# Attention by pairs of heads, side by side in the TensorE array, in one core's decoder step

## What is computed

```python
def sparse_core(q, k_sel, v_sel, valid):   # 8 heads of 64
    s = einsum("bthd,btkhd->bthk", q, k_sel) * 64 ** -0.5
    p = softmax(where(valid, s, -inf)); return einsum("bthk,btkhd->bthd", p, v_sel)
def mem_attend(qm, mk, mv):                # 4 heads of 128, 256 memory tokens
    s = einsum("bthd,bmhd->bthm", qm, mk) * 128 ** -0.5
    p = softmax(s); return einsum("bthm,bmhd->bthd", p, mv)
```

## Time and profile before

| what | value |
|---|---|
| median of 3 runs | 2982.36 us (2980.09 to 2985.59) |
| the profiled execution | 2974.08 us |
| its span, first to last instruction | 2972.5 us |
| mean granted TensorE clock | 0.988 of full speed |
| attention in the profile | about 1610 to 1947 us from the start of the span |

### The profile page before, as it was taken

How to read it: one execution, slowest core, us unless ns; L and a number is a source line. 1 busy time by engine, 2 the same in 40 slices (tenths; PEclk the granted TensorE clock), 3 DMA queues, 4 the chain that set the end, 5 groups by cost and what they waited for, 6 DMA issues and landing times. The chain is left out here.

```text
span 2972.5 us, 56828 instructions
## 1 busy us (share of the span) xinstructions
PE 2844.4 (96%) x21242; PEld 2709.4 (91%) x21242; DVE 2341.1 (79%) x3873; ACT 1236.1 (42%) x2373; POOL 1137.3 (38%) x808
## 2 busy tenths in 40 slices
PE   6999989999999999999988999999989999899999
PEld 6999989999899999999986777799889999899999
DVE  8888897777758999999985666547378888977776
ACT  5444444444433333233445555521344443443443
POOL 4555545554543331113321000021355555454552
PEclk8999999999999999999998999999999999999999
DMA  4333323332232222223128777634533333233331
GB/s 160 93 93 93 104 75 93 93 92 87 86 80 87 87 87 75 85 58 95 59 89 298 265 238 253 227 121 137 148 101 99 100 93 101 75 103 98 95 98 57
DMA packets 359407, 340.35 MB, mean 114 GB/s; under 512 B 16831, under 2 KB 293666, under 8 KB 359134
## 3 DMA queue, kind: packets, MB, share of 16 engines
q1 hardware_dynamic: 354430, 330.41, 35.9%
q0 software_dynamic: 4128, 4.20, 0.5%
q10 hardware_dynamic: 576, 2.10, 0.2%
HBM read 299.60 MB, written 37.05 MB: 113 GB/s over the span
## 5 line engine op out<-in xcount | busy, mean ns | idle before, releaser
L294 PE MATMUL bank<-op_r_ffn,w_hi 128*128 128x256 f32 (+1 forms) x2992 | 580.8, 292 | 32.4 <-DVE op_r_ffn L275 18.2
L294 PEld LDWEIGHTS bank<-op_r_ffn,w_hi 128*128 128x128 f32 x2992 | 475.5, 191 | 39.1 <-issue 36.5
L294 PE MATMUL bank<-op_r_ffn,w_lo 128*128 128x256 f32 (+1 forms) x1496 | 433.5, 290 | 0.0
L294 PE MATMUL bank<-h_hi,w_hi 128*128 128x362 f32 (+1 forms) x1272 | 422.2, 332 | 6.8 <-ACT qi L2024 2.6
L435 POOL TENSOR_TENSOR w_lo<-sums_ffn,w_hi 128x512 fp32r<-128x512 f32 x214 | 317.7, 1494 | 264.5 <-ACT w_hi L431 264.5
L294 PE MATMUL bank<-h_lo,w_hi 128*128 128x362 f32 (+1 forms) x1272 | 417.9, 329 | 0.0
L294 PE MATMUL bank<-h_hi,w_lo 128*128 128x362 f32 (+1 forms) x1272 | 417.8, 328 | 0.0
L294 PE MATMUL bank<-op_r_ffn,more_hi_ffn 128*128 128x288 f32 (+1 forms) x1936 | 375.0, 291 | 13.9 <-ACT s_ffn L575 5.3
L294 PEld LDWEIGHTS bank<-op_r_ffn,more_hi_ffn 128*128 128x128 f32 x1936 | 306.3, 190 | 17.8 <-issue 8.5
L435 POOL TENSOR_TENSOR more_lo_ffn<-sums_ffn,more_hi_ffn 128x512 fp32r<-128x512 f32 x138 | 203.2, 1480 | 226.4 <-ACT more_hi_ffn L431 226.4
L294 PEld LDWEIGHTS bank<-op_r_ffn,w_lo 128*128 128x128 f32 x1496 | 286.0, 191 | 0.0
(11 more groups left out here) (429 smaller groups left out, 7141.8 us busy)
## 6 DMA issues: line engine op xcount, KB each, us to landing
raw<-in_w_ffn_in SPq DMA_DIRECT2D x132, 512.0 KB, 3.9
raw_ffn<-in_w_ffn_out SPq DMA_DIRECT2D x88, 512.0 KB, 3.5
v_ring<-in_cache_v SPq DMA_DIRECT2D x128, 256.0 KB, 4.7
raw<-in_w_in SPq DMA_DIRECT2D x53, 512.0 KB, 4.9
raw_ffn<-in_w_ffn_in SPq DMA_DIRECT2D x44, 512.0 KB, 3.8
kt_two<-in_cache_k SPq DMA_DIRECT2D x88, 256.0 KB, 3.6
kept_g<-stage SPq DMA_DIRECT2D x24, 544.0 KB, 3.1
gate<-kept_g SPq DMA_DIRECT2D x24, 544.0 KB, 3.7
```

The source lines that it names most:

```text
L294: mm = pe.matmul(out, left, right, start=(start and i == 0 and j == 0), stop=(stop and i == n - 1 and j == 2))
```

## The change

A step is now a "double": one query tile with two heads (prompt), or two query tiles with one head (memory). There are 48 of them, and 12 of them are two heads with their memory part.

- Scores: the two heads stand in the upper and lower 64 rows of the array (`tile_position=(e * DH, 0)`), each with its own banks (0 and 1, or 2 and 3). Three products (high by high, high by low, low by high) take the place of two per head. All four banks belong to one double, and the scores of a double wait for the reading of the one just before it.
- Values: the two heads stand in the left and right 64 columns of the array (`tile_position=(0, e * DH)`), the values being the stationary operand now and 128 columns of transposed probabilities the moving one. The output comes out transposed, so that `oturn` falls away.
- The reciprocals of the row sums have to be transposed instead. DVE takes the reciprocals (entry `invert`), copies them over 64 or 128 columns each (`inv`), PE transposes that (entry `inverse`, one block, or two for memory), ACT or DVE copies it to `inv_t`, and DVE multiplies the output by it.
- Turns come one step after the scores, where they came two steps after, and values two steps after, where they came three steps after. They take banks 4 and 7, and 1 and 3 too where these are free.
- The sample's operations: one sample per 6 doubles, in three places of a step: between scores and values, between values and turns, and after the turns' exponential.
- The parts of queries and keys are made for two heads at once, over 128 rows. `vp` has one buffer. Scratch tiles of the stage before (`spread_q`, `mk_sq`) are moved, and the first branch products of the merge wait for other semaphores.

```diff
-    jobs = []
-    for h in range(H):
-        jobs += [("att", i, h) for i in (0, 7, 1, 6, 2, 5, 3, 4)] + [("mem", h % 2 * 4 + i, h // 2) for i in range(4)]
+    doubles = []
+    for hp in range(H // 2):
+        doubles += [("att", i, 2 * hp) for i in (0, 7, 1, 6, 2, 5, 3, 4)] + [("mem", 2 * m, hp) for m in range(4)]
     slots = [
-        [],
-        [("sc", 0)],
-        [("sc", 1)],
-        [("sc", 2)],
-        [("sc", 3)],
-        [("sc", 4), ("smax",)],
-        [("soft",), ("msc",)],
-        [("pt", 0), ("pt", 1), ("pt", 2), ("pt", 3), ("pt", 4)],
-        [("pv",), ("mpt",)],
-        [("mpv",), ("ot",)],
-        [("mot",)],
-        [],
+        ([], [("sc", 0)], []),
+        ([("sc", 1)], [("sc", 2)], []),
+        ([("sc", 3)], [("sc", 4), ("smax",)], []),
+        ([], [("soft",), ("msc",)], []),
+        ([("pt", 0), ("pt", 1), ("pt", 2), ("pt", 3), ("pt", 4)], [("pv",)], [("mpt",)]),
+        ([("mpv",)], [("ot",)], [("mot",)]),
...
+    def sample(d, place):
+        if d < n:
+            for e in slots[d % 6][place]:
+                add(d, e[0], d // 6, *e[1:])
+
+    n = len(doubles)
+    add(0, "queries", 0)
+    add(0, "keys", 0)
+    for d in range(n + 2):
+        if d < n:
+            add(d, "scores", d)
+            following = d // 12 + 1
+            if d % 12 == 8 and following < H // 2:
+                add(d, "queries", following)
+            if d % 12 == 9 and following < H // 2:
+                add(d, "keys", following)
+        sample(d, 0)
+        if 0 <= d - 2 < n:
+            add(d, "values", d - 2)
+        if n <= d:
+            add(d, "merge", 2 + 2 * (d - n))
+        sample(d, 1)
+        if 0 <= d - 1 < n:
+            blocks = 2 * (doubles[d - 1][1] + 1) if doubles[d - 1][0] == "att" else 4
             for g in range(0, blocks, 4):
-                add("turn", s - 2, g, min(4, blocks - g))
-        if s < n:
-
-            add("exp", s)
-            following = s // 12 + 1
-            if s % 12 == 8 and following < H:
-                add("keys", following)
-            for e in slots[s % 12]:
-                add(e[0], s // 12, *e[1:])
-            if s % 12 == 7 and following < H:
-                add("queries", following)
-    return jobs, plan
+                add(d, "turn", d - 1, g, min(4, blocks - g))
+            add(d, "invert", d - 1)
+        if d < n:
+            add(d, "exp", d)
+        sample(d, 2)
+        if 0 <= d - 1 < n:
+            add(d, "inverse", d - 1)
+        if d == n - 1:
+            add(d, "merge", 0)
+            add(d, "merge", 1)
+        elif d == n:
+            add(d, "merge", 3)
...
+    vp = place("vp", [P, 8, P], F32, 0)
+    vn = place("vn", [DEC_T, 512], F32, 4096)
...
+    pb = [place("pb_even", [P, SEQ], F32, 32768), place("pb_odd", [P, 2 * SEQ], F32, 36864)]
...
+    for entry, turn, step in plan:
+        if entry[0] == "scores" and wide(step):
+            held_at[step] = {b: held[b] for b in (1, 3) if b in held}
+        if turn is None:
+            continue
+        free = (4, 7) if wide(step) or step < 2 or step >= n - 3 else (4, 7, 1, 3)
...
+        elif kind == "inverse":
+            d = entry[1]
+            w = 1 if doubles[d][0] == "att" else 2
+            if d >= 1:
+                eng.wait_ge(normed, d)
+            copy(inv_t[:, 0:w, :], b[:, 0:w * P].rearrange("p (e n) -> p e n", e=w)).then_inc(evicted[me], 1)
...
+    def values_of(sp, hp):
+        if hp == 0:
             after_heads(sp, "heads_summed")
-        if j >= 2:
-            sp.wait_ge(valued, last_of["att", 2 * j - 3] + 1)
+        else:
+            sp.wait_ge(valued, last_att(hp - 1) + 1)
         v_rows = O["new_v_prompt"][0, 0].rearrange("(t p) h d -> p t (h d)", p=P)
-        sp.dma_start(vp[:, j % 2, :, :], v_rows[:, :, j * P:(j + 1) * P]).then_inc(vp_in[j % 2], 16)
+        sp.dma_start(vp[:, :, :], v_rows[:, :, hp * P:(hp + 1) * P]).then_inc(vp_in, 16)
...
+                d = s
+                what, i, h = doubles[d]
+                if d >= 1:
+
+                    pe.wait_ge(*scores_read(d - 1))
                 if what == "mem":
-                    if s == 8:
+                    if d == 8:
                         pe.wait_ge(mk_gained, 1)
-                    mm = pe.matmul(bank[b0][:, 0:N_MEM], qmT[:, h, i * P:(i + 1) * P], mkT[:, h, :],
-                                   start=True, stop=True)
+                    for e in range(2):
+                        mm = pe.matmul(scores_of(d, e), qmT[:, h, (i + e) * P:(i + e + 1) * P], mkT[:, h, :],
+                                       start=True, stop=True)
                 else:
                     keys = (i + 1) * P
                     if i == 0:
-                        pe.wait_ge(k_low, 2 * (h + 1))
-                        pe.wait_ge(q_low, h + 1)
+                        pe.wait_ge(q_low, h // 2 + 1)
+                        pe.wait_ge(k_low, h // 2 + 1)
                     for c, k0 in enumerate(range(0, keys, 512)):
                         w = min(512, keys - k0)
-                        out = bank[b0 + c][:, 0:w]
-                        pe.matmul(out, qq[:, i * P:(i + 1) * P], kk_hi[:, k0:k0 + w], start=True, stop=False)
-                        mm = pe.matmul(out, qq[:, i * P:(i + 1) * P], kk_lo[:, k0:k0 + w], start=False, stop=True)
+                        if c:
+                            for t in held_at[d].values():
+                                wait_turn(pe, t)
+                        for m, (q_, k_) in enumerate(((q_hi, k_hi), (q_hi, k_lo), (q_lo, k_hi))):
+                            for e in range(2):
+                                r = slice(e * DH, (e + 1) * DH)
+                                mm = pe.matmul(bank[2 * e + c][:, 0:w], q_[r, i * P:(i + 1) * P], k_[r, k0:k0 + w],
+                                               start=(m == 0), stop=(m == 2), tile_position=(e * DH, 0))
...
                     for j in range(i + 1):
-                        mm = pe.matmul(bank[6][:, 0:DH], pt[:, j, :], vp[:, h // 2 % 2, j, h % 2 * DH:(h % 2 + 1) * DH],
-                                       start=(j == 0), stop=(j == i))
+                        for e in range(2):
+                            r = slice(e * DH, (e + 1) * DH)
+                            mm = pe.matmul(bank[6][r, 0:P], vp[:, j, r], pt[:, e * (i + 1) + j, :], start=(j == 0),
+                                           stop=(j == i), tile_position=(0, e * DH))
...
+            elif kind == "inverse":
+                d = s
+                pe.wait_ge(spread, d + 1)
+                for e in range(1 if doubles[d][0] == "att" else 2):
+                    mm = pe.transpose(tb[:, e * P:(e + 1) * P], inv[:, e, :], ident[:, :])
                 mm.then_inc(turned, 1)
             elif kind == "sc":
...
+    def split_low(dve, hp):
+        dve.wait_ge(q_high, hp + 1)
+        dve.tensor_tensor(q_lo[:, :], qT[:, hp, 0:SEQ], q_hi[:, :].bitcast(F32), ALU.subtract).then_inc(q_low, 1)
+        dve.wait_ge(k_high, hp + 1)
+        dve.scalar_tensor_tensor(k_lo[:, :], kT[:, hp, 0:SEQ], gains[:, 0:1], k_hi[:, :].bitcast(F32),
+                                 ALU.mult, ALU.subtract).then_inc(k_low, 1)
...
+            elif kind == "invert":
+                d = s
+                c = col(d, 0)
+                dve.wait_ge(exped, 2 * d + 2)
+                if d >= 1:
+                    dve.wait_ge(turned, turn_of[("inverse", d - 1)] + 1)
+                dve.reciprocal(rinv[:, c:c + 2], rsum[:, c:c + 2]).then_inc(inverted, 1)
+                dve.wait_ge(inverted, d + 1)
+                if doubles[d][0] == "att":
+                    dve.tensor_copy(inv[:, 0, :].rearrange("p (e n) -> p e n", e=2),
+                                    rinv[:, c:c + 2].unsqueeze(2).to_broadcast([P, 2, DH])).then_inc(spread, 1)
+                else:
+                    dve.tensor_copy(inv[:, :, :], rinv[:, c:c + 2].unsqueeze(2).to_broadcast([P, 2, P])).then_inc(spread, 1)
...
+                dve.wait_ge(valued, d + 1)
+                wait_turn(dve, turn_of[("inverse", d)])
+                to, w = (qT[:, h // 2, i * P:(i + 1) * P], P) if what == "att" else (qmT[:, h, i * P:(i + 2) * P], 2 * P)
+                dve.tensor_tensor(to, bank[6][:, 0:w], inv_t[:, :, :].rearrange("p e n -> p (e n)")[:, 0:w], ALU.mult).then_inc(normed, 1)
```

More of the change, by code:

```diff
@@ L2827, in attention_plan, with add @@
     turns = 0
-    def add(*entry):
+    def add(step, *entry):
         nonlocal turns
         turn = None
-        if entry[0] in ("turn", "oturn", "pt", "mpt", "ot", "mot"):
+        if entry[0] in ("turn", "inverse", "pt", "mpt", "ot", "mot"):
             turn = turns
             turns += 1
[L2835 to L2840, removed]
-        if s < n:
[L2842 to L2858, removed]
-            for g in range(0, blocks, 4):
-                add("turn", s - 2, g, min(4, blocks - g))
-        if s < n:
-            add("exp", s)
-            following = s // 12 + 1
-            if s % 12 == 8 and following < H:
```

(39 more changed lines are left out.)

304 lines of the change are left out of this document (130 added, 174 removed).

## The result

| | before | after |
|---|---|---|
| median of the timed runs, side by side on one chip | 2981.23 us (2975.26 to 2985.59, 4 runs) | 3004.03 us (3001.89 to 3005.60, 4 runs) |
| ratio after / before | | 1.008, 95% interval 1.0068 to 1.0093 |
| span of the profiled execution | 2972.5 us | 3000.3 us |
| mean granted clock of the profiled execution | 0.988 | 0.984 |
| first scores to first merge product, in the profile | 1610.4 to 1939.9: 329.5 us | 1610.6 to 1967.3: 356.8 us |

The changed kernel is slower by 22.8 us (0.8%). In the profiles all of the difference, 27.3 of 27.8 us, lies in attention.

What follows compares the result with a forecast made beforehand. Attention was taken as bound by PE, the PE, DVE, ACT chain close behind. Terms +13 (stage), -1.5, +2 and +1 gave +14.5 on 2974.1, 2988.6; with 8.3 for the median, 2997 us, range 2956 to 3026.

Steps and rivals of the forecast that it cites:

- rival 3: Attention: idle stretches in 12 places each bring a spell at the 1.2 GHz clock, +12 us, 3009 us; chance 0.10.
- PE's work: Attention, per two heads: PE's work falls from 73 to 64.3 us by values, scores and changes of array division.
- Values: Prompt values: two heads' passes run side by side, 72 pairs at 0.11 us, -7.9 us per two heads.
- Scores with their changes of division: Prompt scores: three sets of passes for four, -2.2 us per two heads; all changes of array division together, +1.4.
- the question that I left between two values: Score weight loads of two half-tiles: overlapping they give 8.6 us over the kernel, queued only 2.2.
- Rival 4: Attention: the array's halves don't run side by side, +26 us for scores and +32 for values, 3055 us; chance 0.05.
- The new wait: Before `inverse`, PE waits 1.35 us for DVE's copy, reciprocal and copy; with other waits 19 us per two heads.
- step 9: Tenth of each 12 steps: ACT needs 7.6 us where PE has 3.5, so PE waits 4.1 us.
- step 2: Third of each 12 steps: PE waits 1.7 us for ACT's exponential and 2.3 for `smax`, 4.0 together.
- the fourth key group: Sample's key load: about 7 us of lead against some 6 of issue and landing; 0 to +8, taken as +1.
- Ends of the stage: Attention's start, up to the first `pv`, -1.5 us; its end, with merge operations on ACT and low parts, +2 us.
- Rival 1: Attention: DVE and ACT run ahead, waits stay near 12 us per two heads, 2969 us (2949 without more waits); chance 0.25.

Runs made afterwards that it cites:

- values_in_line: Changed kernel with the prompt's values of the first head all ahead of those of the second, same products: 3017.87 us, ratio 1.0133 to the kernel before.
- filler: Changed kernel with 2 to 20 unread identity transposes per step put on PE ahead of the wait for the reciprocals: 3006.18 us, ratio 1.0084 to the kernel before.
- late_two_banks: Changed kernel with the reciprocals' transposes one step later and memory doubles' scores alternating between banks 0 and 2: 2969.50 us, ratio 0.9961 to the kernel before.
- late_inverse: Changed kernel with the transposes of the reciprocals one step later, between the next scores and values: 2986.18 us, ratio 1.0025 to the kernel before.
- scores_in_line: Changed kernel with the first head's three score products all ahead of the second's, per 512 key columns: 3007.72 us, ratio 1.0081 to the kernel before.
- copy_twice: Changed kernel with DVE copying the prompt doubles' reciprocals to `inv` twice (32 more copies of 0.227 us): 3020.59 us, ratio 1.0136 to the kernel before.

## Why the prediction was right, and where it was short

The forecast was 2997, slower, in a range of 2956 to 3026; it is 3004, between the forecast and the 3009 of rival 3, the clock. Against the kernel before, +14.5 was forecast and +22.8 measured.

**PE's work.** Forecast -8.7 per two heads, measured -8.8 at full clock. Values were forecast at -7.9, and their share of the sum over starts goes from 20.5 to 12.9, -7.6. Scores with their changes of division: forecast -2.2 and part of +1.4; measured 12.1 to 10.9. The pace is as put there, 0.23 for 512 columns of both heads:

```profile
1750.99 0.19 PEld L3185 LDWEIGHTS bank<-k_low,q_high 64*128 64x128 f32 x2
1751.23 0.19 PEld L3185 LDWEIGHTS bank<-k_high,q_low 64*128 64x128 f32 x2
1751.46 0.19 PEld L3185 LDWEIGHTS bank<-k_high,q_high 64*128 64x128 f32 x2
1751.69 0.19 PEld L3185 LDWEIGHTS bank<-k_low,q_high 64*128 64x128 f32 x2
1751.80 0.19 PEld L3185 LDWEIGHTS bank<-k_high,q_low 64*128 64x128 f32 x2
```

These rows decide the question that I left between two values. In the last two rows the pair of one product starts 0.11 us after the pair of the one before: two half-tiles of 128 columns go in what one full load took the earlier trace rows. The Trainium skill, "TensorE: Matmul & The Clock Gate", section "LDWEIGHTS (loading the stationary operand)", has a load's time go with its columns and not its rows. Whether or not that rule holds for each load, the two don't queue. Rival 4 is out: for the scores by these rows, for the values by what taking their overlap away cost, some 16 us (values_in_line).

**The new wait.** Forecast: 1.35 us basic, some 55 us for all `inverse`. Measured from the start of PE's last operation ahead of `inverse` to that of `inverse`, less one pass of 0.11, 48 times: 54.9 us. By step: 3 and 6 forecast 1.4, measured 1.4; 10 and 11 1.2, measured 1.3; 8 2.7, measured 2.6; 4, 5 and 7 0.9, measured 0.9, 0.3, 0.9. In step 9, 4.1 forecast; 1.5 and 1.6 in the rows above, 1 less. Two other terms were wrong and about cancel, which is luck. In step 2, I had 1.7 for `sc` 4 behind ACT's exponential and 2.3 for `smax`, 4.0 together; PE waits 1.4 for `inverse` and 0.3 for ACT's copy, some 9 us less over the stage. Against that the fourth key group, put at +1 from 0 to 8, costs 8.9 (6.8 and 2.1, four places of 1.5 to 3.5 us; before there was no such wait): the lead of 7 us over 6 of issue and landing was too thin.

**What was short: the clock.** I priced it as a rival, at +12 for the stage, and kept it out of the forecast. In the profile 47.6 us are at the 1.2 GHz level where 13.6 were, in nine spells instead of three that begin in the stage (the last of each runs on past its end). The six in mid-stage begin in or shortly behind a stretch of 1.8 to 2.7 us in which PE started nothing, though not every such stretch is followed by one. One of them, the 12 us around the two waits of steps 8 and 9:

```profile
1762.00:1774.00 12.00, 6.53 (x50) 4.46 (x48) 7.98 (x14) 7.41 (x17) 0.00 (x0) 0.86 0.79 257
```

What a spell makes longer is the work in it (the transposes above, 0.20 apart instead of 0.12), not the waiting for another engine. The distances from start to start, waits left out, sum to about 18 us in the eight spells ahead of the merge's products, against 3.2 in two before, and half of the difference, about 7 us, is lost. The timed runs point the same way. Of 107 executions of 13 kernels each has a span and a mean clock; within a kernel, one that has 0.001 less clock is 2.1 us longer (correlation -0.77). The kernel before has 0.9866 on the mean of 41, the changed one 0.9817 of 4: 10 us by that slope, an estimate. So the clock makes up 7 to 10 of the 22.8 us, by estimate, and with the forecast's 14.5 that is about the result. Two caveats: a slope within kernels isn't an experiment on the clock, since a run that waits longer can have a lower clock for that very reason, and filler, which was to be one, didn't move it enough. I count this part as supported, not as shown.

**Where the rest went.** Ends of the stage: forecast -1.5 and +2, in the profiles +2.1 to the first `pv` (in it stands one of the waits for a key page, 3.5 us) and +2.7 after the last (the last `inverse` waits 2.7, and the first merge product 3.9 for POOL's low part, where it waited 1.2). So in the profiles, where the difference is 27.3 us and not 22.8, the ends took 4 us more than forecast and the clock 7, which is most of the excess over 14.5. DVE's 46 us per two heads came out at 45.4; it isn't a bound by volume.

**The sign.** Rival 1 (faster) was to turn at 15.7 us of waits per two heads, in the forecast's way of counting. late_two_banks is that rival made true by two edits, some 12 us faster than the kernel before, a third of the 35 that no more waits than before would have given. The later `inverse` alone wasn't enough for the sign (1.0025, with an interval above 1); it took the second bank as well.

## What to carry to other kernels

When a faster form of a product needs a small product more (here a transposed reciprocal), ask what PE does between the last operation that it waits for and that product; if nothing stands between, the whole way to another engine and back (here 1.4 us) is paid each time. Put it a step later than its inputs, but look at once at the wait that is next: late_inverse alone brought half of what both edits did, and its partner, a second bank for the memory scores, was worth little alone and much with it. And add the clock to the sum of idle stretches: here, by an estimate that no experiment confirms, it came on top with 7 to 10 of 22.8 us.

## What was not expected of the hardware

- Matmuls of the upper and lower half of the array ran side by side although the program had one head's three products of a tile ahead of the other's (scores_in_line, pairs 0.01 us apart). For the left and right halves, the order in the program did matter (values_in_line: 0.11 per pair against 0.09 each).
- The granted clock varies from run to run of one kernel (0.984 to 0.990 before), and the span with it, 2.1 us for each 0.001. More than half of the scatter between runs of a kernel goes with it (correlation -0.77); which of the two drives the other isn't shown.
- PE waited for the same end of DVE's chain whether it was idle or did some 40 us of other work in front of it (filler).
- An edit that puts 7.4 us of DVE work into the chain cost PE 10 us of waits, and the kernel about 16 (copy_twice).
